# Prompt attention, two heads a step: the copy of the turned blocks moved ahead of the exponentials in ScalarE's order

## What is computed

```python
def block(args):                      # one query block of 128 rows, latent heads
    s = (q_nope @ k_nope + q_rope @ k_rope) * scale          # float32
    s = where(kpos <= qpos, s, NEG_INF)
    p = exp(s - max(s)) / sum(exp(s - max(s)))
    return p @ v
# window heads: the same with (window, dilation) = (128,1), (512,4), (2048,16);
# the three softmaxes are merged by their denominators
```

## Time and profile before

| | |
|---|---|
| median of 3 runs | 1310.25 us (1310.02 to 1311.48) |
| the profiled execution | 1311.06 us, of which the profile's span is 1309.3 us |
| prompt attention (S(0) to the last PV) | about 342 to 458 us of the span |
| TensorE busy, whole span | 1204.9 us (92%) |
| VectorE, ScalarE busy, whole span | 581.0 us (44%), 478.6 us (37%) |
| chain that ended last | PE 86%, DVE 8%, ACT 3%, issue 2% |

### The profile page before, as it was taken

The page is one execution under the profiler, slowest core; times in us unless marked ns, Lnnn a source line. Parts: engine busy times, 40 slices in busy tenths (PEclk is TensorE's granted clock), DMA queues, the critical chain, the costliest instruction groups (busy, mean ns, idle before and its releaser), DMA issues.

```text
span 1309.3 us, 21517 instructions
## 1 busy us (share of the span) xinstructions
PE 1204.9 (92%) x8308; PEld 1007.5 (77%) x8308; DVE 581.0 (44%) x1031; ACT 478.6 (37%) x829; POOL 45.7 (3%) x60
## 2 busy tenths in 40 slices
PE   4999989999988799999999789799999999999698
PEld 3997977333556576666677478799999999999698
DVE  4313321453575576666666364632333233333643
ACT  4223233211355455555555432433321122222332
POOL 0000000232000000000000000000000000000000
PEclk8999999976788799999999879899999999999899
DMA  6675413002348247777777112364662354562122
GB/s 235 237 257 177 139 46 92 10 1 87 129 161 292 71 137 243 245 244 234 247 231 217 48 49 98 113 222 147 216 227 95 136 210 159 208 226 100 43 78 88
DMA packets 68815, 202.66 MB, mean 155 GB/s; under 512 B 7457, under 2 KB 40226, under 8 KB 67394
## 3 DMA queue, kind: packets, MB, share of 16 engines
q1 hardware_dynamic: 66562, 131.74, 30.9%
q0 software_dynamic: 2176, 69.90, 14.9%
HBM read 196.53 MB, written 72.13 MB: 205 GB/s over the span
## 4 chain that ended last, share of the span: by engine, by line
PE 86%; DVE 8%; ACT 3%; issue 2%; DMA 0%; SPq 0%; DVEq 0%; ACTq 0%
PE ps L497 50%; PE ps L1045 13%; PE ps L390 4%; PE ps L401 3%; PE ps L1012 2%; PE ps L413 2%; PE ps L1022 2%; PE ps L1033 2%; DVE R L438 2%; DVE tmp L455 1%; PE ps L1102 1%; PE ps L1096 1%; DVE aLo L356 1%; PE ps L1061 1%; PE ps L936 1%
## 5 line engine op out<-in xcount | busy, mean ns | idle before, releaser
L497 PE MATMUL ps<-aHi,wHi 128*128 128x272 f32 (+1 forms) x1392 | 296.0, 294 | 38.5 <-DVE aLo L356 35.1
L497 PE MATMUL ps<-aHi,wLo 128*128 128x272 f32 (+1 forms) x1392 | 291.8, 292 | 0.0
L497 PE MATMUL ps<-aLo,wHi 128*128 128x272 f32 (+1 forms) x1392 | 291.1, 291 | 0.0
L497 PEld LDWEIGHTS ps<-aHi,wHi 128*128 128x128 f32 (+1 forms) x1392 | 220.0, 189 | 48.9 <-issue 19.5
L369 DVE TENSOR_TENSOR wLo<-ring,wHi 128x1024 fp32r<-128x1024 f32 (+3 forms) x105 | 133.4, 1271 | 211.5 <-ACT wHi L364 211.4
L497 PEld LDWEIGHTS ps<-aLo,wHi 128*128 128x128 f32 (+1 forms) x1392 | 221.2, 190 | 0.0
L497 PEld LDWEIGHTS ps<-aHi,wLo 128*128 128x128 f32 (+1 forms) x1392 | 220.2, 190 | 0.0
L364 ACT ACTIVATE wHi<-ring 128x1024 fp32r<-128x1024 f32 (+3 forms) x105 | 114.5, 1091 | 196.1 <-PE ps L497 196.1
L1328 DVE TENSOR_REDUCE ssq<-att 128x8 f32<-128x512 f32 x128 | 87.4, 683 | 89.1 <-ACT att L767 88.3
L767 ACT ACTIVATE att<-ps 128x512 f32<-128x512 f32 x128 | 76.4, 597 | 114.6 <-PE ps L1045 114.0
L1045 PE MATMUL ps<-wkHi,pgHi 128*128 128x512 f32 x256 | 103.2, 403 | 8.2 <-ACT att L767 7.0
(11 more groups left out here) (190 smaller groups left out, 1419.8 us busy)
## 6 DMA issues: line engine op xcount, KB each, us to landing
out_o_cv<-in_cv POOLq DMA_DIRECT2D x16, 2044.0 KB, 8.2
ring<-in_wgu SPq DMA_DIRECT2D x44, 512.0 KB, 3.5
big<-in_pgt SPq DMA_DIRECT2D x128, 144.0 KB, 2.2
big<-in_pgl SPq DMA_DIRECT2D x128, 128.0 KB, 2.4
kv<-in_ck SPq DMA_DIRECT2D x8, 1792.0 KB, 8.0
ring<-in_win SPq DMA_DIRECT2D x21, 512.0 KB, 4.4
kv<-in_cv SPq DMA_DIRECT2D x8, 1024.0 KB, 5.8
kv<-in_cv SPq DMA_DIRECT2D x24, 256.0 KB, 6.2
```

The source lines that it names most:

```text
L497: ins = nc.tensor.matmul(pair[rows, a, 0:HT], w[:, c], xx[:, k, a * HT:(a + 1) * HT], start=(k == 0 and z == 0), stop=(k == nk - 1 and z = ...
```

## The change

In ScalarE's order of the prompt attention, C(n-2) with its two waits stands ahead of E(n) with its wait, instead of behind it. No instruction is added or removed, and no other engine's order, wait, buffer or DMA is touched. The cast at n = 6 still comes after both.

```diff
             for n in range(len(units) + LAG_T):
+                if n >= LAG_T:
+                    m = n - LAG_T
+                    w = (units[m][1] + 1) * P
+                    act.wait_ge(a_t, m + 1)
+                    if m >= 2:
+                        act.wait_ge(a_pv, m - 1)
+                    act.activation(prT[m % 2][:, :, 0:w], ps[1][:, :, 0:w], ACT.Copy).then_inc(a_tc, 1)
                 if n < len(units):
                     w = (units[n][1] + 1) * P
                     act.wait_ge(a_nm, n + 1)
                     for z in range(2):
                         pr = probs_of(n, z)[:, 0:w]
                         last = act.activation(pr, pr, ACT.Exp, bias=st[:, n % 3, NEGM, z:z + 1],
                                               accum_out=st[:, n % 3, SUM, z:z + 1])
                     last.then_inc(a_e, 1)
-                if n >= LAG_T:
-                    m = n - LAG_T
-                    w = (units[m][1] + 1) * P
-                    act.wait_ge(a_t, m + 1)
-                    if m >= 2:
-                        act.wait_ge(a_pv, m - 1)
-                    act.activation(prT[m % 2][:, :, 0:w], ps[1][:, :, 0:w], ACT.Copy).then_inc(a_tc, 1)
```

## The result

| | before | changed |
|---|---|---|
| median | 1310.87 us (4 runs, 1310.02 to 1311.76) | 1298.86 us (4 runs, 1298.46 to 1300.53) |
| profiled execution, its span | 1311.06, 1309.3 us | 1300.53, 1298.8 us |
| ratio | | 0.9911, 95% interval 0.9894 to 0.9928 |

The change makes the kernel 12.0 us faster by the medians. (The ratio is estimated from all runs of both kernels, so it is not quite the quotient of the medians.) I had forecast 1294.0, 16.2 us less, within 1288.5 to 1300.5. The profiled execution of the changed kernel is the slowest of its four.

The account below looks back on a forecast made before the run. TensorE bounds the attention, held by waits for ScalarE's copies and a lowered clock. 20 us at full clock (11.2 less about 2 order, some 11 clock) minus 3.8 for slow places gives 16.2: 1294.0 us, range 1288.5 to 1300.5.

Parts of the forecast that it names:

- The waits for copies: TensorE's T waits on ScalarE's copies: seven of 1.2 us (8.3) and 2.9 us elsewhere would go.
- Late exponentials cost nothing: ScalarE's exponentials, now behind the copy, have 0.7 to 0.9 us of cover each; delay costed at 0.
- The pair-by-pair sum: Prompt attention, T(i = 2) starts carried forward at full clock: stage ends at 438.1 instead of 458.17, gain 20 us.
- What the order alone gives: Prompt attention without any clock change: 8.3 + 2.9 = 11.2 us, less about 2 that VectorE takes back.
- The clock in this stage: Attention: some 11 of the 20 us come from fewer half-clock stretches; 3.8 us of slow stretches kept.
- two slow places: Stretches staying slow: the 32 small matmuls at n = 24, about 1.1 us, and behind the new scores, 2.7 us.
- The rival of a fully granted clock: Attention keeps full clock everywhere: gain 20 us, 1290 us; chance 0.2.
- The rival in which the clock falls as often as before: Attention keeps as many slow stretches: gain 9 to 12 us, 1299 us; chance 0.2.
- behind 458 us ... I cost it at 0: After the attention the work is the same and starts earlier, so no cost: 0 us.
- the forecast itself: Whole kernel with one to three slow stretches left: range 1291.5 to 1297.5 us, chance 0.54.
- Slower: Rival: exponentials become late on ScalarE, all copies' 2.7 us a pair join the chain: +11, 1321 us; chance 0.03.
- no change: Rival: another release, such as R, takes the copy's place at T, so no gain: 1310 us; chance 0.03.

Follow-up runs that it names:

- experiment 5: Changed kernel with an extra ScalarE copy ahead of each step's exponentials: 0.45 us a step, 1299.85 us, ratio 0.9888; 1.0 us a step, 1307.24 us, ratio 0.9945.
- run A of experiment 3: Kernel before with the copy put ahead of the exponentials only in steps with n mod 4 = 3: 1307.42 us, ratio 0.9959.
- experiment 4: Kernel before, old ScalarE order, with six extra matmuls filling TensorE's wait ahead of T(i = 2) in pairs 0 to 4 and 6: 1306.64 us, ratio 0.9952.
- experiment 2: Changed kernel, unaltered, measured a second and a third time: 1299.36 us, ratio 0.9905, and 1298.46 us, ratio 0.9899.
- experiment 6: Changed kernel with VectorE's R(n-1) ahead of the maxima of n in steps with i = 3: 1303.68 us, ratio 0.9912.
- run B: Kernel before with the copy put ahead of the exponentials in steps with i = 0, 1, 2 and behind them at i = 3: 1313.85 us, ratio 1.0002.

## Why the prediction came out as it did

**The waits for copies: right.** Seven times 1.2 us (8.4, put down as 8.3) and 2.9 elsewhere were to go, and all waits of T for copies went. T(i = 2) starts 0.06 us behind R, a little less than the 0.14 that I took.

**Late exponentials cost nothing: right, and shown.** R nowhere waits for E in the changed kernel, and the cover is between 0.45 and 1.0 us a step (experiment 5).

**The pair-by-pair sum: right to 0.2 us while the clock was full.** Counted from the start of the first scores (341.53 there, 344.14 in the changed kernel), T(i = 2) of pairs 0 to 4 was to come at 9.9, 20.7, 33.8, 44.6 and 54.5 us; it came at 10.0, 20.7, 33.9, 44.6 and 54.5 (starts 354.16, 364.86, 378.01, 388.71, 398.66). VectorE bounds between pairs 1 and 2 as said: 13.15 us, forecast 13.1.

**What the order alone gives: right.** Where the clock was full throughout, the time from one T(i = 2) to the next hardly differs between executions, and the orders can be compared without the clock (us, by pairs; a dash where a half-clock stretch fell):

| | 0 to 1 | 1 to 2 | 2 to 3 | 3 to 4 |
|---|---|---|---|---|
| before, two profiles | 11.94, 11.94 | -, 13.92 | 11.99, 11.94 | -, - |
| before with waits filled | 11.92 | 13.92 | 11.94 | 11.69 |
| run A of experiment 3 | 10.70 | 13.92 | 11.94 | 10.64 |
| changed, three profiles | 10.69 to 10.70 | 13.15 to 13.16 | 10.69 to 10.70 | 9.95 to 9.96 |
| changed, exponentials 0.45 us late | 10.70 | 13.15 | 10.70 | 9.99 |

In the changed kernel's first profile the third of these ends at the T(i = 2) shown with the result, 388.71, and begins here:

```profile
378.01 0.87 PE L1022 MATMUL ps<-C,att 128*128 128x128 f32 x6 [1.15 <-DVE att L1285]
```

The order is worth 1.2 us in a latent pair, as forecast, 0.8 where VectorE bounds, and 1.7 in the window pair (there against the filled waits; 9.9 was the forecast for this pair). Filling the waits does not change the first three, so what it gave in experiment 4 is the clock's.

**The clock in this stage: right.** I kept 3.8 us for two slow places. The sum at full clock ends the stage at 96.6 us and it ended at 100.7: 4.1 us. That the two agree to 0.3 us is partly luck. The stretches lay at the small matmuls (409.1 to 415.9) and at the last pair (439.8 to 443.2), where I had said that the last pairs should be near 1.00; the one expected behind the new scores came in the third profile only (423 to 426.4). The rival of a fully granted clock would be 96.6, and the second profile came near it, 97.1, helped by an earlier rise of the clock at its start (T(i = 2) of pair 0 at 8.9 us instead of 10.0). The rival in which the clock falls as often as before fell: 37 and 25 us at half clock before, and 17, 8 and 10 in the changed kernel. Between profiles that start alike, at 345.2 to 345.5 us and at half clock until 350, the attention took 111.6 us before, 108.4 with the waits filled and 97.1 in the changed kernel. The stage gain was 16.0 in the first profiles and 15.5 between the means (98.6 of three, 114.1 of two), but single pairings of the two kernels give 10.9 to 19.6, so that it came out at the forecast's 16.2 is chance as well.

**What failed is the term "behind 458 us ... I cost it at 0", and its unspoken twin ahead of the attention.** They measured +2.9 and +2.6 us in the first pair of profiles. They are no work of the change that a transfer or a wait shows. The instructions are the same and the first 250 us behind the attention are equal. What differs is where the clock is granted, in stages that the change does not touch: by 4 us ahead of the attention between executions of one kernel, and behind it as experiment 2 has it. I carried the stage's gain to the whole kernel as if those stages stood still. The median gained 12.0 us, and 13.1 and 15.9 in the two repetitions (by the ratios 11.7, 12.5 and 13.3, each under the forecast 16.2). The median of 1298.9 us lies within my range, but outside the 1291.5 to 1297.5 that I gave to the forecast itself, and next to the 1299 of the rival whose mechanism fell. So the mechanism of the stage is confirmed, and the closeness of the total is not. A sum over one stage of such a kernel needs a few us on either side for them.

**Slower, and no change,** the other rivals, fell: the first by experiment 5, the second by the waits. But the second's mechanism, another release right behind the one removed, is what run A of experiment 3 and experiment 6 met.

The rule of the Trainium skill (TensorE: Matmul & The Clock Gate, "What's actually happening") that activity releases the throttled clock agrees with experiment 4: idle time filled with work that nobody reads brought the clock from 0.84 and 0.89 to 0.95, and the kernel down by 0.5%. The waits that remained, up to 2.9 us, did not all draw a fall.

## What to carry to other kernels

In an in-order engine put the short step that frees a shared buffer ahead of the long step whose result is wanted later, and work out the cover of the long one: here it held 0.45 us a step and not 1.0. When several waits of one kind follow in a ring, the one that ends last hides the others; judge a partial fix by the next wait of the ring, not by the one removed. With a gated clock, one profile gives a stage only to some us: take two of each kernel, compare stage by stage, and count the slow stretches before putting a difference down to the edit. Best of all, compare a piece that ran at full clock in both.

## What the runs showed of the hardware

Extra matmuls in waits make this kernel faster, in the old order by 0.5% (0.9952, interval 0.9925 to 0.9979), without changing the pace of a pair at full clock (11.94 us with and without). The clock can fall with TensorE busy: the 32 matmuls of 64 rows and 32 columns (L984) took 4.9 us in the changed kernel's first profile against 3.6 before, and the clock was at 0.51 from 409 us on, with the engine busy for the whole stretch. In ten of the twelve profiles the clock falls during these matmuls or within 1.4 us of their end; in the third profile of the changed kernel and in run B it does not. That their small size is the cause is not shown. And an unchanged kernel's attention took 116.6 us in one execution and 111.6 in another, with the same waits, by where the slow stretches fell.
